# A gated recurrence on one core: relu bounds and first products on ScalarE, all four differences of a level on GpSimd

## What is computed

```python
def forget_gates(z, lb):
    f = lb + (1.0 - lb) * jax.nn.sigmoid(z)
    log_f = jnp.log(jnp.maximum(f, F_MIN))
    k = (1.0 - lb) * jax.nn.sigmoid(-z)
    return k, log_f

def step(S, inp):                       # one chunk, all heads; run forwards and backwards
    qc, kc, vc, gc = inp
    b = jnp.cumsum(gc, axis=2)
    o_inter = jnp.einsum('bhtk,bhkv->bhtv', qc * jnp.exp(b), S)
    diff = jnp.where(tri[:, :, None], b[:, :, :, None, :] - b[:, :, None, :, :], NEG_BIG)
    a = jnp.einsum('bhtk,bhsk,bhtsk->bhts', qc, kc, jnp.exp(diff))
    o = o_inter + jnp.einsum('bhts,bhsv->bhtv', a, vc)
    b_last = b[:, :, -1]
    S = jnp.exp(b_last)[..., None] * S + jnp.einsum('bhsk,bhsv->bhkv', kc * jnp.exp(b_last[:, :, None] - b), vc)
    return S, o
```

## Time and profile before

| | us |
|---|---|
| median of 3 runs | 2776.69 (2776.19 to 2777.66) |
| the profiled execution, its own time | 2781.77 |
| its span | 2780.0 |
| busy: TensorE | 2676.1 (96%) |
| busy: VectorE | 1824.2 (66%) |
| busy: ScalarE | 1412.7 (51%) |
| busy: GpSimd | 564.4 (20%) |
| granted TensorE clock, mean | 0.984 |

### The profile page before, as it was taken

How to read it: one execution, slowest core, us unless ns; L and a number is a source line. 1 busy time by engine, 2 the same in 40 slices (tenths; PEclk the granted TensorE clock), 3 DMA queues, 4 the chain that set the end, 5 groups by cost and what they waited for, 6 DMA issues and landing times.

```text
span 2780.0 us, 44757 instructions
## 1 busy us (share of the span) xinstructions
PE 2676.1 (96%) x18308; PEld 2148.3 (77%) x18308; DVE 1824.2 (66%) x2299; ACT 1412.7 (51%) x1783; POOL 564.4 (20%) x488
## 2 busy tenths in 40 slices
PE   9999999999999999994999999999999999999997
PEld 7888888878888778872777777777777777777775
DVE  7212232778999666566767767766776776677788
ACT  3112222867664433322656655665665666566674
POOL 2000030005554333320001100110001110111435
PEclk9999999999999999996999999999999999999999
DMA  7478876776465653426778787887887788778983
GB/s 246 167 209 243 268 241 152 158 280 229 162 222 199 219 198 117 140 81 243 287 277 306 284 305 278 303 291 277 298 310 286 278 294 316 286 288 322 362 325 129
DMA packets 237452, 686.26 MB, mean 247 GB/s; under 512 B 18729, under 2 KB 65208, under 8 KB 232128
## 3 DMA queue, kind: packets, MB, share of 16 engines
q1 hardware_dynamic: 220480, 630.58, 63.7%
q0 software_dynamic: 16768, 52.82, 7.1%
HBM read 577.46 MB, written 105.88 MB: 246 GB/s over the span
## 4 chain that ended last, share of the span: by engine, by line
PE 49%; DVE 1%; DMA 1%; POOL 1%; issue 1%; ACT 0%; ACTq 0%; DVEq 0%; POOLq 0%
PE moe_strip L2561 12%; PE moe_up L2576 4%; PE moe_gate L2576 4%; PE moe_gate L2578 4%; PE moe_up L2577 4%; PE moe_gate L2577 4%; PE moe_up L2578 4%; PE moe_down L2576 4%; PE moe_down L2577 4%; PE moe_down L2578 4%; DMA out<-moe_norm_x 1%; DVE pieces_low L2769 1%; PE moe_up L2502 1%; PE moe_turn L2536 0%; PE moe_gate L2511 0%
## 5 line engine op out<-in xcount | busy, mean ns | idle before, releaser
L2769 DVE TENSOR_TENSOR pieces_low<-pieces_raw,moe_high 128x1024 fp32r<-128x1024 f32 x768 | 893.0, 1217 | 355.5 <-PE moe_strip L2561 345.8
L2661 ACT ACTIVATE moe_high<-pieces_raw 128x1024 fp32r<-128x1024 f32 x768 | 769.6, 1052 | 361.5 <-PE moe_up L2578 195.7
L2561 PE MATMUL moe_strip<-pieces_raw,moe_xT_p 128*32 128x256 f32 x4096 | 230.4, 383 | 1.0 <-ACT moe_xT_p L2673 1.0
L2561 PEld LDWEIGHTS moe_strip<-pieces_raw,moe_xT_p 128*32 128x32 f32 x4096 | 130.5, 111 | 96.8 <-issue 14.0
L2576 PE MATMUL moe_gate<-moe_high,moe_xT 128*128 128x512 f32 x512 | 202.3, 395 | 1.9 <-DVE pieces_low L2769 1.7
L2576 PE MATMUL moe_up<-moe_high,moe_xT 128*128 128x512 f32 x512 | 203.0, 396 | 0.2 <-issue 0.2
L2576 PE MATMUL moe_down<-moe_high,moe_hdn 128*128 128x512 f32 x512 | 202.5, 396 | 0.0
L2578 PE MATMUL moe_gate<-pieces_low,moe_xT 128*128 128x512 f32 x512 | 199.7, 390 | 0.0
L2577 PE MATMUL moe_up<-moe_high,moe_xT 128*128 128x512 f32 x512 | 199.6, 390 | 0.0
L2577 PE MATMUL moe_down<-moe_high,moe_hdn 128*128 128x512 f32 x512 | 199.5, 390 | 0.0
L2577 PE MATMUL moe_gate<-moe_high,moe_xT 128*128 128x512 f32 x512 | 199.5, 390 | 0.0
(11 more groups left out here) (375 smaller groups left out, 5707.2 us busy)
## 6 DMA issues: line engine op xcount, KB each, us to landing
pieces_raw<-in_w_gate_e SPq DMA_DIRECT2D x128, 1024.0 KB, 6.0
pieces_raw<-in_w_up_e SPq DMA_DIRECT2D x128, 1024.0 KB, 8.8
pieces_raw<-in_w_down_e SPq DMA_DIRECT2D x128, 1024.0 KB, 4.9
bias_fx<-xs SPq DMA_DIRECT2D x40, 1024.0 KB, 5.4
fr_raw<-in_w_in SPq DMA_DIRECT2D x16, 1024.0 KB, 9.2
ws<-fr_late_split SPq DMA_DIRECT2D x32, 512.0 KB, 4.6
bias_fw<-ws SPq DMA_DIRECT2D x32, 512.0 KB, 7.7
mo_gates<-h SPq DMA_DIRECT2D x20, 512.0 KB, 4.3
```

What stands on the lines that cost most here:

```text
L2561: last = nc.tensor.matmul(strip_ps[j * CP:(j + 1) * CP, kind, :], x, raw[g % RAW][:, k * D + j * STRIP:k * D + (j + 1) * STRIP], start=sta ...
L2661: nc.scalar.activation(high[:, g % HI, cols], raw[g % RAW][:, cols], ACT.Copy).then_inc(hi_done, 1)
L2769: nc.vector.tensor_tensor(low[g % RAW][:, cols], raw[g % RAW][:, cols], high[:, g % HI, cols].bitcast(F32), ALU.subtract).then_inc(lo_done, 1)
```

## The change

Four edits, all in `stage_recurrence`:

1. GpSimd computes all four differences of each level; VectorE's `differences` is gone, and ScalarE's wait for it.
2. The upper part of the split gate is made by ScalarE for heads 1 to 3, as `Relu(omlb * sigmoid + (lb - 2^-60))` into `lf`, ahead of the Identity that makes `f`; the logarithm adds the 2^-60 back as its bias. VectorE's `clamp` keeps only the lower part. For head 0 VectorE still makes both.
3. The products 0 are copied whole from PSUM into `A` by ScalarE (`open_pairs`, between exp 2 and the second half of the key copies) instead of being multiplied by the identity on VectorE; every entry off the diagonal is overwritten by a later gather. The wait for the store of the last head's `A` moves with it.
4. Two small tiles (`lb_over`, `split`) are set up once by VectorE, and the semaphore counts follow.

```diff
-    SETUP, PER = 5 + 3 + MASKS, 3 * 2
+    SETUP, PER = 5 + 2 + 3 + MASKS, 3 * 2
...
                 def difference(hd, r):
                     pool.wait_ge(scanned, hd * 2 + min(r + 1, 2))
                     wait_slot(pool, hd, r)
-                    for to, a, b in exponents(r)[:3]:
+                    for to, a, b in exponents(r):
                         last = nc.gpsimd.tensor_tensor(to, a, b, ALU.subtract)
                     last.then_inc(pool_d, 1)
...
                         for g, (a, count) in enumerate(CHUNK_GROUPS):
-                            before = (hd * NL + n - 1) * NG + g + 1
-                            if before > 0:
-                                pe.wait_ge(a_done, before)
+                            if n == 1:
+                                pe.wait_ge(a_opened, hd * NG + g + 1)
+                            elif hd + n > 0:
+                                pe.wait_ge(a_done, (hd * LEVELS + max(n - 1, 0) - 1) * NG + g + 1)
...
                     for d in range(2 if p else 0):
-                        one_less, least = (x[:, d, p:p + 1] for x in (omlb, lb))
+                        one_less, least, over = (x[:, d, p:p + 1] for x in (omlb, lb, lb_over))
                         act.wait_ge(z_opened, (p - 1) * 2 + d + 1)
+                        nc.scalar.activation(lf[:, d], f[:, d], ACT.Relu, bias=over, scale=one_less)
                         nc.scalar.activation(f[:, d], f[:, d], ACT.Identity, bias=least, scale=one_less)
                         nc.scalar.activation(k[w][:, d], k[w][:, d], ACT.Copy, scale=one_less).then_inc(z_done, 1)
...
-                        nc.scalar.activation(lf[:, d], lf[:, d], ACT.Ln)
+                        nc.scalar.activation(lf[:, d], lf[:, d], ACT.Ln, bias=split[:])
...
                     else:
-                        act.wait_ge(dve_d, hd * LEVELS + r - 1)
                         nc.scalar.activation(W[:, r % WS], W[:, r % WS], ACT.Exp).then_inc(exp_done, 1)
+
+                def open_pairs(hd):
+
+                    if hd >= 1:
+                        act.wait_ge(o_stored, 16 * hd)
+                    for g, (a, count) in enumerate(CHUNK_GROUPS):
+                        act.wait_ge(l_mm, hd * NL * NG + g + 1)
+                        nc.scalar.activation(A[:, a * P:(a + count) * P], l_ps[g][:, 0:count * P], ACT.Copy)\
+                          .then_inc(a_opened, 1)
...
                         if r == 2:
+                            open_pairs(hd)
                             copy_keys(hd, 1)
                             evict(units_until((hd, "keys")))
...
+                nc.vector.tensor_scalar(lb_over[:], lb[:], LN_SPLIT, None, ALU.subtract).then_inc(chain, 1)
+                step.next()
+                nc.vector.memset(split[:], LN_SPLIT).then_inc(chain, 1)
+                step.next()
...
-                def clamp(d, count):
-
-                    nc.vector.tensor_scalar(lf[:, d], f[:, d], LN_SPLIT, None, ALU.max).then_inc(chain, 1)
-                    dve.wait_ge(chain, count)
+                def clamp(d):
+
                     nc.vector.tensor_scalar(f[:, d], f[:, d], F_MIN, LN_SPLIT, ALU.max, ALU.min).then_inc(clamped, 1)
...
-                        clamp(d, count_of.next())
+                        nc.vector.tensor_scalar(lf[:, d], f[:, d], LN_SPLIT, LN_SPLIT, ALU.max, ALU.subtract)\
+                          .then_inc(chain, 1)
+                        dve.wait_ge(chain, count_of.next())
+                        clamp(d)
...
-                    def differences(r):
-                        if r >= 2:
-                            wait_slot(dve, hd, r)
-                            to, a, b = exponents(r)[3]
-                            nc.vector.tensor_tensor(to, a, b, ALU.subtract).then_inc(dve_d, 1)
...
                             dve.wait_ge(l_mm, (hd * NL + n) * NG + g + 1)
-                            if n == 0:
-                                if hd >= 1:
-                                    dve.wait_ge(o_stored, 16 * hd)
-                                nc.vector.tensor_tensor(chunked(A[:, cols]), chunked(l_ps[g][:, 0:width]),
-                                                        ident[:].unsqueeze(1).to_broadcast([P, count, P]), ALU.mult)\
-                                  .then_inc(a_done, 1)
+                            if n == 1:
+                                dve.wait_ge(a_opened, hd * NG + g + 1)
                             else:
-                                dve.wait_ge(a_done, (hd * NL + n - 1) * NG + g + 1)
-                                nc.vector.copy_predicated(A[:, cols], mask[:, n - 1, 0:width], l_ps[g][:, 0:width])\
-                                  .then_inc(a_done, 1)
+                                dve.wait_ge(a_done, (hd * LEVELS + n - 2) * NG + g + 1)
+                            nc.vector.copy_predicated(A[:, cols], mask[:, n - 1, 0:width], l_ps[g][:, 0:width])\
+                              .then_inc(a_done, 1)
...
-                    differences(2)
...
-                    gather(0)
                     for r in range(2, R):
-                        if r + 1 < R:
-                            differences(r + 1)
                         weights(r)
```

More of the change, by code:

```diff
@@ L907, in stage_recurrence @@
         below = W[:, 0, 1, 512:1024]
-        omlb = s.sb("omlb", [P, 2, HG_HEADS])
+        omlb, lb_over = s.sb("omlb", [P, 2, HG_HEADS]), s.sb("lb_over", [P, 2, HG_HEADS])
+        split = s.sb("split", [P, 1])
         lb_e, lb_r = s.sb("lb_e", [P, 2, HG_HEADS]), s.sb("lb_r", [P, 2, HG_HEADS])
@@ L914, in stage_recurrence @@
         k_in, q_in, v_in = ([first, s.sem(name)] for first, name in zip(head_in, ("k_in1", "q_in1", "v_in1")))
-        (iota_done, q_done, z_done, clamped, ln_done, scanned, dec_done, pool_d, dve_d,
+        (iota_done, q_done, z_done, clamped, ln_done, scanned, dec_done, pool_d,
          exp_done, w_ready, qi_done, ki_turned, ki_copied, l_mm, a_done, ds_mm, s_made, o_mm, o_copied,
@@ L918, in stage_recurrence @@
              "iota_done", "q_done", "z_done", "clamped", "ln_done", "scanned",
-             "dec_done", "pool_d", "dve_d", "exp_done", "w_ready", "qi_done", "ki_turned", "ki_copied", "l_mm",
+             "dec_done", "pool_d", "exp_done", "w_ready", "qi_done", "ki_turned", "ki_copied", "l_mm",
              "a_done", "ds_mm", "s_made", "o_mm", "o_copied", "chain", "lb_ready"))
-        z_opened = s.sem("z_opened")
+        z_opened, a_opened = s.sem("z_opened"), s.sem("a_opened")
         ki_groups = [(0, a, n) for a, n in CHUNK_GROUPS] + [(1, a, n) for a, n in reversed(CHUNK_GROUPS)]
@@ L1153, in head @@
                             fill((hd, "pairs", n))
-                    pe.wait_ge(a_done, (hd + 1) * NL * NG)
+                    pe.wait_ge(a_done, (hd + 1) * LEVELS * NG)
                     pe.wait_ge(s_made, (hd + 1) * NS)
@@ L1322, in prepare_first @@
                         dve.wait_ge(chain, count_of.next())
-                        clamp(d, count_of.next())
+                        nc.vector.tensor_scalar(lf[:, d], f[:, d], LN_SPLIT, LN_SPLIT, ALU.max, ALU.subtract)\
+                          .then_inc(chain, 1)
+                        dve.wait_ge(chain, count_of.next())
+                        clamp(d)
                 def prepare(p, d):
                     dve.wait_ge(z_done, p * 2 + d + 1)
-                    clamp(d, SETUP + PER + (p - 1) * 2 + d + 1)
+                    clamp(d)
                 def run_sums(p):
```

## The result

The changed kernel takes 2796.89 us (median of 4 runs, 2795.15 to 2798.76) beside 2777.18 us (median of 4, 2776.19 to 2779.49) of the kernel before: ratio 1.0070, 95% interval 1.0057 to 1.0082, so 19.7 us more. Its profiled execution ran for 2798.76 us with a span of 2797.0 us and a mean granted clock of 0.980.

The account below looks back on a forecast made before the run. TensorE's gaps were taken as the bound; heads 0 to 3 at 6.0 + 2.5 + 3.5 - 1.5 = +10.5 us and clock +4.1 gave +14.6 on 2776.7: 2791.3, say 2791 us, range 2769 to 2802.

Parts of the forecast that it names:

- The bound: Four heads: TensorE's gaps set the kernel's length nearly one for one; a faster VectorE could give at most 20.5 us.
- Exponential 3: ScalarE, first levels: starts later as GpSimd's four subtractions alternate with VectorE, 3.3 us in head 0, 2.9 head 2, 0.7 head 1.
- The Relus: ScalarE's gates: two more activations a head, 2.7 us, between 2.3 and 7.8 us, in the chain before the evictions.
- The evictions: Filler units' PSUM evictions behind the gates: come later and move TensorE by +6.0, +2.75 and +5.1 us in heads 0, 1, 2.
- VectorE's relief: Waits for VectorE that go: heads 0 to 2 become +6.0, +2.5 and +3.5 us, head 3 gains 1.5 us.
- Products 5 in head 1: TensorE waits about 4 us there, as late `weights(6)` meets GpSimd's difference 8 (+3.3 us by alternation).
- The head ends: TensorE's wait at the end of each head stays near 2.3 us, behind gather 6, the next head's scans and gather 7.
- Clock: Four new or grown TensorE waits over 2 us lead to slow spells: 4 x 0.6 x 1.7 = +4.1 us.
- Relief: Rival: exponential 3 is not late and VectorE's waits and slow spells go; net -7.5 us, 2769 us; chance 17%.
- the change would balance out: Rival: exponential 3 late by half the count, head ends shrink, no new slow spells; +4.4 us, 2779 us; chance 24%.
- GpSimd as the bound of the short levels: Rival: four subtractions make products 6 and 7 wait 2 us each in three heads; +12 us, 2803 us; chance 12%.
- No table came with the Relus: Rival on ScalarE: Relu brings table loads, +5 us a head, 2806 us; chance 3%.

## Why the prediction was right, and where it was not

**The bound.** TensorE's gaps set the time: +14.0 us of named waits, 14.3 us of idle time and 6.6 us more of busy time at the lower clock make up the 20.8 us of the heads. Right. That 20.5 us at most could be won was not tested; nothing was won.

**Exponential 3.** Predicted 3.3 us late in head 0, 2.9 in head 2, 0.7 in head 1. It came 2.4 us later in head 0 by the table above; counted from the output products before the head, 18.22 instead of 15.21 us in head 2 (+3.0) and 18.15 instead of 17.65 in head 1 (+0.5). The mechanism is right and head 0's size 0.9 us too large. In its working I needed both edits, the fourth subtraction and the missing diagonal products; the table shows that the subtraction alone is enough, as far as one execution of that kernel can.

**The Relus.** 2.7 us a head, no table load, and the whole of it in front of the evictions: measured 2.7, and 2.7 again with two other activations in their place. The rule of the Trainium skill that relu belongs on VectorE (ScalarE: Activation LUTs, Rules for kernel authors) holds here twice over. I compared the Relu's form with VectorE's mean of 1.37 us and called it weak agreement; but that mean has GpSimd's disturbance in it, and undisturbed VectorE's bound is a good deal shorter than the Relu's 1.45 us:

```profile
751.59 0.81 DVE L1308 TENSOR_SCALAR hg_lf<-hg_f 128x1280 f32<-128x1280 f32 x1
```

And the place in ScalarE's list is dear.

**The evictions.** Their delay: predicted +6.0, +3.4 and +5.6 us, measured +5.5 (of which 0.4 is head 0's later start), +3.2 and +5.7 (the last two from the head's output products: 36.95 for 33.74, 37.01 for 31.32). Right. What TensorE paid for it: predicted shifts of 6.0, 2.75 and 5.1, measured waits of 6.43, 4.55 and 7.35. **This is the term that was mis-sized**, in heads 1 and 2: I took 0.65 and 0.5 us of slack off the delay and left the moment of TensorE's need as it was. It came 1.9 and 2.0 us earlier after the head's output products (33.1 for 34.96 us, 30.4 for 32.4), because before both heads began with a slow spell, about 1.7 us, and had 0.15 and 0.29 us of waits for state sums, and now neither had any of it. That time was not gained but turned into wait.

**VectorE's relief.** The state sums' 3.1 us went, and head 3, for which I had -1.5, came out at 0.0: its waits went, and 12 us at a granted clock of 0.86 behind the 2.55 us wait took their place. Products 5 in head 1 wait 4.37 us (predicted: about 4), and for the reason that was given, a late `weights(6)` that runs beside GpSimd; two added activations alone bring the same wait (4.36). In head 2 the 2.01 us went and 0.73 came back. The head ends were to stay near 2.3 us each and are 2.54, 0.20 and 2.55; in head 1 TensorE came to it late, from the 4.37 us wait and products 5 at 4.61 us instead of some 2.4, so that this is no relief either.

**Clock.** Predicted 4 x 0.6 x 1.7 = 4.1 us. The chance was too low, since all four waits of over 4 us led to a spell, and the spells are longer than those behind waits of 2 us. TensorE's extra busy time is 6.6 us. Head by head my sums of +6.0, +2.5, +3.5 and -1.5 with 4.1 of clock on top became +7.5, +6.6, +6.8 and 0.0: 20.8 us in place of 14.6.

**The rivals.** Relief did not win: exponential 3 was late by most or all of the count, and with all relief and early evictions the kernel was still 0.37% slower than before. That the change would balance out is what one mended variant does (no Relus, early evictions, 1.0010), not the change. My sum for this rival was wrong as well: +4.4 on 2776.7 is 2781, not 2779. GpSimd as the bound of the short levels falls largely: TensorE's waits for gathers grew by 0.9 us, not by some 12. Its upper end was too low, 7.5 us for four subtractions, where my own count for head 0 had 8.8 and 8.5 were measured; it falls all the same, although ScalarE waits 28.7 us for GpSimd in 11 places, which I had named as a sign against the forecast. Those waits have cover, except when something is moved so that it meets them, as exponential 4 was. No table came with the Relus.

**What stays open.** Why early evictions cost the kernel before 0.14%; why the costs of the edits do not add; and how much of the change's loss is clock rather than wait, since no run holds the one and changes the other.

## What to carry to other kernels

An engine at half load can still be the bound, through what stands in its list: before work is moved onto it, find the PSUM evictions and other short releases behind that point, and take their slack as the price; 8.1 us of activations on ScalarE cost 8.6 us here by the medians, 7 to 13 by the interval. Work taken off an engine that was 92% busy gained nothing here, where an order, and not the engine, ends the waits. And a slack read next to a stretch at the slow clock is not there once that stretch is gone.

## What the runs showed of the hardware

- Waits of TensorE of 4.4 to 7.4 us were each followed by a granted clock of 0.65 to 0.76 in a window of 10 to 14 us around and behind them, while behind waits of 2.0 to 2.3 us it is 0.72 over 6 us or 0.79 over 8 us, and only in three of five cases. In the changed kernel one wait of 2.54 us was followed by full clock and one of 2.55 us by 0.86 over 12 us.
- Taking the diagonal product (one operand in PSUM, one in SBUF, 0.68 us) off VectorE made GpSimd slower: it had held VectorE for 1.6 us in head 0 without contending. What took its place reads two SBUF tensors and contends (1.90 us for a difference that takes 0.82 alone); exponential 3 of head 0 was 0.7 to 1.2 us later from that alone.
